# One core, two transformer blocks: convolution-branch gates ahead of the latents' up products

## The chip, the cores and the metric

The kernel runs on one core of one Trainium2 chip. Its time is the device time of one execution in microseconds (us). The engines are TensorE (PE; PEld is its weight load), VectorE (DVE), ScalarE (ACT), GpSimd (POOL) and SyncE (SP, which only issues DMAs here).

## What is computed

512 tokens of width 1024 go through two layers of a first block and then two layers of a second. The change is in the first block only:

```
def _layer(x, mem, positions, w_in, ...):
    proj = x @ w_in
    (aq, ak, av, ag, bcq, bckv, bkr, bg, cq, ck, cv, cg, mq, mg) = jnp.split(proj, _split_points(), axis=-1)
    ya = _banded_chunk_attention(aq, ak, av, A_PREV_CHUNKS, rel_bias=rel_bias)
    yb = _mla(bcq, bckv, bkr, positions, mla_q_norm, w_uq, mla_kv_norm, w_ukv)
    yc = _banded_chunk_attention(rope(cq), rope(ck), cv, SWA_PREV_CHUNKS, sinks=swa_sinks)
    ym = _memory_attention(mq, mem, w_mem_kv)
    gated = jnp.concatenate([ya * silu(ag), yb * silu(bg), yc * silu(cg), ym * silu(mg)], axis=-1)
    return _layer_norm(alpha * x + gated @ w_out, ln_gain, ln_bias)
```

`_mla` (branch B) normalises the latents `bcq` and `bckv`, multiplies them by `w_uq` and `w_ukv` (the up products), turns 32 of each query head's 96 rows by the rotary tables, and attends. Branch C is called the convolution branch in the change's title; its gate is `cg`, branch B's is `bg`.

## The kernel before

Everything is kept transposed (features on partitions, 512 tokens along the free axis). Each float32 product is three matmuls on a high and a low part (`r3`, line 554): a product of a 128x128 weight block with 512 tokens is one k part, 3 matmuls, and a projection tile of 128 features is 8 of them.

Weights come in chunks of two tiles. SP loads a chunk into one of two buffers `w_stage`, ACT rounds it into `w_hi` (line 1049, in halves), POOL makes `w_lo` (line 540, 8 pieces), and PE's `begin_chunk` waits for both. Chunks 10, 11 and 12 of a layer hold the up products' weights (`CHUNK_U`), the C gates (`CHUNK_CG`) and the B gates (`CHUNK_BG`).

Attention of a layer is a pipeline of 32 pairs of heads by query tile: steps 0 to 7 belong to branch A, 8 to 15 to M (memory), 16 to 23 to C, 24 to 31 to B, and two more steps drain it. In step t PE issues the scores of pair t (line 602), for every fourth step the spread of the head sums (line 640), the value products of pair t-2 (line 616), the transposes of pair t-1 (line 626), and then the step's share of other work. DVE takes the masked maximum of pair t (lines 1548, 1556 or 1553) and then copies the transposes of pair t-1 out of PSUM (line 1531); ACT takes the exponentials (line 1096). Scores of pair t need the PSUM bank that the copy of pair t-2 frees.

The other work is cut by hand into units: three in each of steps 0 to 3, two in each later step, so that step t above 3 has units 12 + 2(t - 4) and the one after. `b1_units` lists them; PE's, ACT's and DVE's `later_projections` are generators written to match. A number n in ACT's or DVE's `until(n)` means that what follows runs at unit n, behind that engine's attention work of the unit's step and ahead of that of the next step. All units' results go to two PSUM banks in turn, and PE's `acquire` waits until ACT (`evac`, line 1116) or DVE has taken what was there before.

Before the change the units are: cv up to 29; `uk` (keys of B) at 30 and 31, with the transposes of cv at 32; `uv` (values) 33 and 34; `uq` (queries) 35 and 36, one empty; `cg0`, `cg1` at 38 to 45 in quarters; `bg0`, `bg1` at 46 to 61 in eighths. The four rotations of the query heads (`rope`, lines 1505, 1507 and 1510, three DVE instructions for each head) run at units 41 and 42. Seven parts of the gated output are rounded and split (`split_out` on ACT, `out_lo` on DVE, lines 1112 and 1579) at units 62 to 65.

Of the kernel before, what the change touches and what calls it, by code (L numbers as in the profile page):

```python
# [20 lines left out]
P = 128  # L21
# [4 lines left out]
TT = TOK // P  # L26
# [36 lines left out]
def segments():  # L63
# [5 lines left out]
    for l in range(DEPTH):  # L69
# [7 lines left out]
        for n, (f0, nf) in enumerate(HALVES):  # L77
            early = 2 if n == 0 else 0
            if early:
# [9 lines left out]
              "bkv", "bq0", "bq1", "ck", "cq0", "cq1", "cv", None, None, None, "cg0", "cg1", "bg0", "bg1"]  # L89
AHEAD = 12  # L90
CHUNK_CQ, CHUNK_CV, CHUNK_U, CHUNK_CG, CHUNK_BG = 8, 9, 10, 11, 12
# [15 lines left out]
def b1_units(l):  # L107
# [139 lines left out]
def build(nc, dram, out):  # L247
# [3 lines left out]
    with ctx:  # L251
# [294 lines left out]
        def _(pe):  # L546
# [146 lines left out]
            def later_projections(l, c0):  # L693
# [36 lines left out]
                c = c0 + CHUNK_U  # L730
                begin_chunk(c)
                pe.wait_ge(S("lat_split"), 3 * l + 3)
                for h in range(4):
                    o = acquire(("uk", l, h))
                    w = slice(768 + h * 64, 768 + h * 64 + 64)
                    r3(o[0:64, :], w_hi[:, c % 2, w], w_lo[:, c % 2, w], lat_h[:, 2, :], lat_l[:, 2, :], True, True, True)
                    if h % 2 == 1:
                        yield
                transpose_all(("tv", l, "cv"), ("w", l, "cv"), qb[:, 2, :])
                yield  # L740
                for t in range(TT):
                    o = acquire(("uv", l, t))
                    w = slice(768 + 256, 768 + 512)
                    r3(o[:, 0:256], lat_h[:, 2, t * P:t * P + P], lat_l[:, 2, t * P:t * P + P], w_hi[:, c % 2, w], w_lo[:, c % 2, w],
                       True, True, True)
                    if t % 2 == 1:
                        yield
                for h in range(4):
                    o = acquire(("uq", l, h))
                    w = slice(h * 96, h * 96 + 96)  # L750
                    w1 = slice(384 + h * 96, 384 + h * 96 + 96)
                    r3(o[0:96, :], w_hi[:, c % 2, w], w_lo[:, c % 2, w], lat_h[:, 0, :], lat_l[:, 0, :], True, False)
                    r3(o[0:96, :], w_hi[0:64, c % 2, w1], w_lo[0:64, c % 2, w1], lat_h[0:64, 1, :], lat_l[0:64, 1, :], False, True, True)
                    if h % 2 == 1:
                        yield
                yield
                yield from pair_of_tiles(CHUNK_CG)
                yield from pair_of_tiles(CHUNK_BG, 8)
# [265 lines left out]
        def _(act):  # L1024
# [93 lines left out]
            for l in range(DEPTH):  # L1118
# [40 lines left out]
                def later_projections():  # L1159
# [45 lines left out]
                    for n in range(2):  # L1205
                        yield from until(30 + n)
                        round_chunk(b1_chunk(l, 11), half=n)
                        for h in (2 * n, 2 * n + 1):
                            evac(("uk", l, h), kb[0:64, h, :], rows=slice(0, 64))
                    yield from until(32)  # L1210
                    token_major(("tv", l, "cv"), vc[:, :, :])
                    for n in range(2):
                        yield from until(33 + n)
                        for t in (2 * n, 2 * n + 1):
                            evac(("uv", l, t), vb[:, t, :], cols=slice(0, 256))
                    for n in range(2):
                        yield from until(35 + n)
                        for h in (2 * n, 2 * n + 1):
                            evac(("uq", l, h), qb[0:96, h, :], rows=slice(0, 96), scale=SCALE_B)
# [878 lines left out]
```

## Time and profile before

| | us |
|---|---|
| three runs | 1737.13, 1739.89, 1739.97 (median 1739.89) |
| the profiled execution | 1740.3 |
| its span, first to last instruction | 1738.5 |
| attention of layer 0, first C scores to the output product | 190.55 to 263.83 |
| attention of layer 1, first C scores to the output product | 491.27 to 567.04 |
| PE busy share of the span | 96% |
| mean granted TensorE clock | 0.978 |

A timeline row gives start, duration, engine, line, operation, result and operands, the number of instructions that are merged in the row, and in brackets how long the engine had been idle and what released it. A matmul's own duration overlaps with the next one, so that work on PE is measured from start to start. A granted clock of 1.00 is TensorE's 2.4 GHz, 0.50 is 1.2 GHz.

### The profile page before, as it was taken

The numbers are of one execution on the slowest core, as the hardware profiler recorded it, in microseconds if no ns is written. First come the engines' busy times: TensorE is split into PE (matmuls) and PEld (weight loads), VectorE is DVE, ScalarE is ACT, GpSimd is POOL, SyncE is SP. The second block draws the span as 40 slices with busy tenths as digits, with TensorE's granted clock in tenths as the row PEclk, the third lists the DMA queues.
The fourth block names the chain that finished last, engine by engine and source line by source line (L and its number), as shares of the span: only waits on it lengthen the run. The fifth ranks groups of instructions, "written<-read, shape, count | busy, mean of one in ns | idle before, by whom it ended". The sixth has DMA issues, their size and how long they took to land.

```text
span 1738.5 us, 23836 instructions
## 1 busy us (share of the span) xinstructions
PE 1668.4 (96%) x8754; PEld 1320.4 (76%) x8754; DVE 786.5 (45%) x1498; ACT 695.0 (40%) x1146; POOL 683.6 (39%) x523
## 2 busy tenths in 40 slices
PE   6999899999999979989999999999998999999999
PEld 5777668787666857868888888888876888888887
DVE  7216664402666265673544115523665355404440
ACT  4344462633445153553433224333454344313431
POOL 3432315343231544425444444344352544344433
PEclk9999999999998979989999999999999999999999
DMA  6321203222120213112222232224221322232222
GB/s 248 107 80 49 80 25 122 96 100 74 50 75 26 85 49 103 51 50 97 97 97 78 91 108 88 91 79 138 86 74 41 105 77 94 90 103 97 97 81 88
DMA packets 26879, 150.68 MB, mean 87 GB/s; under 512 B 3888, under 2 KB 4144, under 8 KB 12912
## 3 DMA queue, kind: packets, MB, share of 16 engines
q1 hardware_dynamic: 23968, 142.78, 24.3%
q10 hardware_dynamic: 2832, 6.84, 1.1%
q8 instruction: 50, 0.82, 0.2%
q14 instruction: 29, 0.24, 0.0%
HBM read 142.66 MB, written 2.10 MB: 83 GB/s over the span
## 4 chain that ended last, share of the span: by engine, by line
PE 85%; DVE 6%; ACT 3%; issue 3%; POOL 2%; DMA 1%; ACTq 0%; DVEq 0%; POOLq 0%
PE ring L554 72%; PE outs L616 3%; PE scores L602 2%; PE ring L602 1%; POOL w_lo L540 1%; PE scores L626 1%; PE ring L640 1%; PE ring L626 1%; PE ring L670 1%; DMA xt<-in_x 1%; DVE tmp L1505 1%; POOL w_fold L532 1%; ACT xt L1267 1%; ACT w_hi L1049 1%; DVE probs_t L1531 0%
## 5 line engine op out<-in xcount | busy, mean ns | idle before, releaser
L540 POOL TENSOR_TENSOR w_lo<-w_stage,w_hi 128x258 fp32r<-128x258 f32 (+5 forms) x471 | 650.0, 1410 | 1010.8 <-ACT w_hi L1049 610.5
L554 PE MATMUL ring<-xh,w_lo 128*128 128x512 f32 x1296 | 519.6, 401 | 19.2 <-DVE w_lo L1463 10.7
L554 PE MATMUL ring<-xh,w_hi 128*128 128x512 f32 x1296 | 514.1, 397 | 0.0
L554 PE MATMUL ring<-xl,w_hi 128*128 128x512 f32 x1296 | 513.8, 396 | 0.0
L554 PEld LDWEIGHTS ring<-xh,w_lo 128*128 128x128 f32 x1296 | 245.5, 189 | 80.7 <-DVE w_lo L1463 10.7
L554 PEld LDWEIGHTS ring<-xh,w_hi 128*128 128x128 f32 x1296 | 246.1, 190 | 55.7
L554 PEld LDWEIGHTS ring<-xl,w_hi 128*128 128x128 f32 x1296 | 246.0, 190 | 53.3
L1394 ACT ACTIVATE w_hi<-w_stage 128x2048 fp32r<-128x2048 f32 (+2 forms) x70 | 116.6, 1666 | 158.2 <-PE ring L554 158.2
L1404 ACT ACTIVATE g<-ring,convw 128x512 f32<-128x512 f32 x88 | 68.1, 778 | 245.4 <-DVE ring L1903 245.4
L1049 ACT ACTIVATE w_hi<-w_stage 128x2064 fp32r<-128x2064 f32 (+2 forms) x81 | 123.4, 1536 | 64.9 <-PE ring L554 64.4
L1885 DVE TENSOR_TENSOR xt<-xt,ring 128x512 f32<-128x512 f32 x48 | 33.0, 688 | 247.3 <-PE ring L554 247.3
L554 PE MATMUL ring<-act_h,w_lo 128*128 128x512 f32 x352 | 139.2, 395 | 0.0
L1903 DVE TENSOR_TENSOR ring<-ring,tmp 128x512 f32<-128x512 f32 x88 | 61.2, 699 | 172.1 <-PE ring L554 161.9
L554 PE MATMUL ring<-act_h,w_hi 128*128 128x512 f32 x352 | 139.0, 395 | 0.0
L554 PE MATMUL ring<-act_l,w_hi 128*128 128x512 f32 x352 | 138.9, 395 | 0.0
L554 PEld LDWEIGHTS ring<-act_h,w_lo 128*128 128x128 f32 x352 | 66.3, 188 | 16.2 <-DVE act_l L1916 0.7
L1096 ACT ACTIVATE probs<-scores,neg_max 128x256 f32<-128x256 f32 (+2 forms) x96 | 50.2, 526 | 71.0 <-DVE neg_max L1550 14.3
L554 PEld LDWEIGHTS ring<-act_h,w_hi 128*128 128x128 f32 x352 | 66.2, 188 | 15.7
L554 PEld LDWEIGHTS ring<-act_l,w_hi 128*128 128x128 f32 x352 | 66.2, 188 | 15.7
L1096 ACT ACTIVATE probs<-ring,neg_max 128x256 f32<-128x256 f32 (+2 forms) x96 | 45.9, 481 | 72.4 <-DVE neg_max L1548 19.6
L1910 DVE SCALAR_TENSOR_TENSOR g<-ring,convw,g 128x511 f32<-128x511 f32 x88 | 66.0, 750 | 12.1 <-DVE g L1908 4.6
L1908 DVE SCALAR_TENSOR_TENSOR g<-ring,convw,g 128x511 f32<-128x511 f32 x88 | 65.2, 741 | 1.0 <-ACT g L1404 1.0
(281 smaller groups left out, 2213.4 us busy)
## 6 DMA issues: line engine op xcount, KB each, us to landing
w_stage<-in_mixed SPq DMA_DIRECT2D x62, 1032.0 KB, 4.8
w_stage<-in_up SPq DMA_DIRECT2D x44, 1024.0 KB, 4.8
w_stage<-in_down SPq DMA_DIRECT2D x16, 768.0 KB, 4.3
w_stage<-in_down SPq DMA_DIRECT2D x16, 640.0 KB, 3.9
xt<-in_x ACTq DMA_DIRECT2D x4, 512.0 KB, 11.4
g<-q SPq DMA_DIRECT2D x16, 128.0 KB, 2.3
out_t<-xt ACTq DMA_DIRECT2D x8, 256.0 KB, 2.0
mem_f<-in_mem SPq DMA_DIRECT2D x1, 1024.0 KB, 9.6
```

The source lines that it names most:

```text
L540: ins = nc.gpsimd.tensor_tensor(w_lo[:, slot, cols], source[:, cols], w_hi[:, slot, cols].bitcast(F32), ALU.subtract)
L554: ins = nc.tensor.matmul(o, lhs, rhs, start=start, stop=stop, skip_group_check=True)
L602: nc.tensor.matmul(acquire(("S", it["n"]))[:, 0:it["nb"] * P], q_of(it), k_of(it, l), start=True, stop=True, skip_group_check=True).then_i ...
L616: ins = nc.tensor.matmul(o_bank[it["o"] % 2][lo:lo + 64, it["qt"] * P:it["qt"] * P + P], v_of(it, l, j), probs_t[:, it["par"], j * P:j * P ...
L626: ins = nc.tensor.transpose(o[:, j * P:j * P + P], probs[:, it["n"] % 3, j * P:j * P + P], ident[:, :])
L1049: ins = A(w_hi[:, c % 2, first:last], source[:, first:last], ACT.Copy)
L1096: A(probs[:, n % 3, 0:w], bank(("S", n))[:, 0:w], ACT.Exp, bias=per_row(neg_max, it), scale=1.0 if it["branch"] == "M" else -1.0, accum_ou ...
L1394: A(w_hi[:, c % 2, 0:width], w_stage[:, c % 2, 0:width], ACT.Copy).then_inc(S("w_hi_done"), 1)
L1404: A(g[:, 4 * s + 2 + v, :], bank((kind, l, f0 + first + s))[:, :], ACT.Identity, bias=convw[:, l, taps, 4 * v + 3:4 * v + 4], scale=convw[ ...
L1903: v.tensor_tensor(bank(name)[:, :], bank(name)[:, :], tmp[:, 0, :], ALU.mult).then_inc(S("normed"), 1)
L1908: step(v.scalar_tensor_tensor(out=cc[:, 1:TOK], in0=hh[:, 0:TOK - 1], scalar=convw[:, l, i * 2 + (f0 + first + s), 4 * c:4 * c + 1], in1=c ...
L1910: v.scalar_tensor_tensor(out=cc[:, 0:TOK - 1], in0=hh[:, 1:TOK], scalar=convw[:, l, i * 2 + (f0 + first + s), 4 * c + 2:4 * c + 3], in1=cc ...
```

## The change

The C gates come ahead of the up products, and the chunks swap places in the weight stream. The units of the up products come in the order uq, uk, uv, one in every second unit with an empty one in front. The first B gate keeps its eighths, the second comes in quarters. There are 64 units where there were 62.

```
@@ the units
-              "bkv", "bq0", "bq1", "ck", "cq0", "cq1", "cv", None, None, None, "cg0", "cg1", "bg0", "bg1"]
+              "bkv", "bq0", "bq1", "ck", "cq0", "cq1", "cv", None, "cg0", "cg1", None, None, "bg0", "bg1"]
-CHUNK_CQ, CHUNK_CV, CHUNK_U, CHUNK_CG, CHUNK_BG = 8, 9, 10, 11, 12
+CHUNK_CQ, CHUNK_CV, CHUNK_CG, CHUNK_U, CHUNK_BG = 8, 9, 10, 11, 12
-    units += [[("uk", l, 0), ("uk", l, 1)], [("uk", l, 2), ("uk", l, 3)], [("tv", l, "cv")]]
-    for name in ("uv", "uq"):
-        units += [[(name, l, 0), (name, l, 1)], [(name, l, 2), (name, l, 3)]]
-    units += [[]]
+    units += [[("tv", l, "cv")], []]
     for t in ("cg0", "cg1"):
         units += [[], [], [], [("w", l, t)]]
-    for t in ("bg0", "bg1"):
-        units += [[]] * 7 + [[("w", l, t)]]
+    for name in ("uq", "uk", "uv"):
+        units += [[], [(name, l, 0), (name, l, 1)], [], [(name, l, 2), (name, l, 3)]]
+    units += [[]] * 7 + [[("w", l, "bg0")]] + [[]] * 3 + [[("w", l, "bg1")]]
@@ ACT
+                    yield from until(30)
                     token_major(("tv", l, "cv"), vc[:, :, :])
+                    yield from round_halves(32, b1_chunk(l, 11))
+                    yield from until(35)
                     evac(w("cg0"), g[:, 4, :])
-                    yield from until(45)
+                    yield from until(39)
                     evac(w("cg1"), g[:, 5, :], ACT.Silu)
+                    for n in range(2):
+                        yield from until(41 + 2 * n)
+                        for h in (2 * n, 2 * n + 1):
+                            evac(("uq", l, h), qb[0:96, h, :], rows=slice(0, 96), scale=SCALE_B)
+                        round_chunk(b1_chunk(l, 12), half=n)
+                    for n in range(2):
+                        yield from until(45 + 2 * n)
+                        for h in (2 * n, 2 * n + 1):
+                            evac(("uk", l, h), kb[0:64, h, :], rows=slice(0, 64))
+                    for n in range(2):
+                        yield from until(49 + 2 * n)
+                        for t in (2 * n, 2 * n + 1):
+                            evac(("uv", l, t), vb[:, t, :], cols=slice(0, 256))
+                    yield from round_halves(52, b1_chunk(l, 13))
                     for t in range(2):
-                        yield from until(53 + 8 * t)
+                        yield from until(59 + 4 * t)
                         evac(w(f"bg{t}"), g[:, 2 + t, :], ACT.Silu)
                     for n in range(7):
-                        yield from until(62 + n // 2)
+                        yield from until(64 + n // 2)
                         split_out(l, n)
@@ DVE
                     for h in range(4):
-                        yield from until(41 + h // 2)
+                        yield from until(46 + h // 2)
                         if h == 0:
                             dve.wait_ge(S("uq_swapped"), 32 * (l + 1))
                         rope(tmp[rr, h, :], qb[rr, h, :], rr, cos32, sin32, [qb[rr, h, :]], "rope_done")
                     for n in range(7):
-                        yield from until(62 + n // 2)
+                        yield from until(64 + n // 2)
                         out_lo(l, n)
```

PE's generator follows the same list; its arithmetic is the same, in another order. Lines of the changed kernel are up to 5 higher on DVE and ACT and 2 lower on PE.

On DVE, before, from the copy of pair 17 to the mask of pair 20 (steps 18 to 20 of layer 0):

```order
L1531 COPY probs_t<-scores 128x256 x2
L1679 TENSOR_TENSOR g<-outs,g 128x512
L1505 TENSOR_TENSOR tmp<-tmp,sin_67 32x512
L1507 TENSOR_TENSOR qb<-qb,cos_66 32x512
L1510 TENSOR_TENSOR qb<-qb,tmp 32x512
L1505 TENSOR_TENSOR tmp<-tmp,sin_67 32x512
L1507 TENSOR_TENSOR qb<-qb,cos_66 32x512
L1510 TENSOR_TENSOR qb<-qb,tmp 32x512
L1556 ISA scores,neg_max<-scores,masks,neg_sink 128x256
```

The same engine in the changed kernel, from the gate of branch C (`scale_gate`, now L1677) on, in step 21:

```order
L1677 TENSOR_TENSOR g<-ring,g 128x512
L1510 TENSOR_TENSOR tmp<-tmp,sin_67 32x512
L1512 TENSOR_TENSOR qb<-qb,cos_66 32x512
L1515 TENSOR_TENSOR qb<-qb,tmp 32x512
L1510 TENSOR_TENSOR tmp<-tmp,sin_67 32x512
L1512 TENSOR_TENSOR qb<-qb,cos_66 32x512
L1515 TENSOR_TENSOR qb<-qb,tmp 32x512
L1510 TENSOR_TENSOR tmp<-tmp,sin_67 32x512
L1512 TENSOR_TENSOR qb<-qb,cos_66 32x512
L1515 TENSOR_TENSOR qb<-qb,tmp 32x512
L1510 TENSOR_TENSOR tmp<-tmp,sin_67 32x512
L1512 TENSOR_TENSOR qb<-qb,cos_66 32x512
```

Units 46 and 47 are both in step 21, so that the rotations, which stood two and two around the mask of pair 19, now stand all four in a row, ahead of the mask of pair 22.

On PE, before, the end of step 15 of layer 0: the values and, right behind, the first query head, with the semaphores that each waits for (`ring_freed0` and `ring_freed1` are the two banks of the units):

```order
L554 MATMUL ring<-w_hi,lat_l 128x256 [waits ring_freed0]
L554 MATMUL ring<-w_lo,lat_h 128x256
L554 MATMUL ring<-w_hi,lat_h 128x256
L554 MATMUL ring<-w_hi,lat_l 128x256 [waits ring_freed1]
L554 MATMUL ring<-w_lo,lat_h 128x256
L554 MATMUL ring<-w_hi,lat_h 128x256
L554 MATMUL ring<-lat_h,w_lo 96x512 [waits ring_freed0]
```

The same engine in the changed kernel, the units of step 22 and the scores behind them:

```order
L552 MATMUL ring<-w_hi,lat_l 128x256 [waits ring_freed0]
L552 MATMUL ring<-w_lo,lat_h 128x256
L552 MATMUL ring<-w_hi,lat_h 128x256
L552 MATMUL ring<-w_hi,lat_l 128x256 [waits ring_freed1]
L552 MATMUL ring<-w_lo,lat_h 128x256
L552 MATMUL ring<-w_hi,lat_h 128x256
L600 MATMUL scores<-kc,qc 128x256 [waits ring_freed4]
```

The query heads no longer follow the values; what follows is the scores of pair 23, which wait for DVE's copy of pair 21 (`ring_freed4`).

On ACT, before, the end of the attention (from the exponential of pair 28 on):

```order
L1096 ACTIVATE probs,row_sum<-ring,neg_max 128x128 x2
L1116 ACT_TABLE_LOAD
L1116 ACTIVATE g<-ring 128x512
L1096 ACT_TABLE_LOAD
L1096 ACTIVATE probs,row_sum<-scores,neg_max 128x256 x2
L1112 ACTIVATE xh<-g 128x512 x4
L1096 ACTIVATE probs,row_sum<-ring,neg_max 128x384 x2
L1112 ACTIVATE xh<-g 128x512 x3
L1096 ACTIVATE probs,row_sum<-scores,neg_max 128x512 x2
```

The same engine in the changed kernel, from the exponential of pair 28 on:

```order
L1101 ACTIVATE probs,row_sum<-ring,neg_max 128x128 x2
L1101 ACTIVATE probs,row_sum<-scores,neg_max 128x256 x2
L1121 ACT_TABLE_LOAD
L1121 ACTIVATE g<-ring 128x512
L1101 ACT_TABLE_LOAD
L1101 ACTIVATE probs,row_sum<-ring,neg_max 128x384 x2
L1117 ACTIVATE xh<-g 128x512 x4
L1101 ACTIVATE probs,row_sum<-scores,neg_max 128x512 x2
```

The last gate with its two table loads and the four splits have moved behind one more exponential, a step later.

## Rows read from the trace of the kernel before

**Rows 1.** The page, part 1: busy time of each engine

```profile
PE 1668.4 (96%) x8754; PEld 1320.4 (76%) x8754; DVE 786.5 (45%) x1498; ACT 695.0 (40%) x1146; POOL 683.6 (39%) x523
```

**Rows 2.** Waits of PE, 430 to 610: total, times, longest

```profile
PE ring L554 <- ACT vc L1154: 0.3, 1, 0.3
```

**Rows 3.** Timeline of PE, layer 1: waits in steps 13 to 21

```profile
477.71 0.44 PE L554 MATMUL ring<-lat_h,w_lo 128*64 128x512 f32 x1 [0.54 <-DVE g L1672]
488.35 0.48 PE L554 MATMUL ring<-lat_h,w_lo 128*96 128x512 f32 x1 [2.08 <-ACT vb L1116]
511.64 0.82 PE L602 MATMUL ring<-kc,qc 64*128 64x128 f32 x4 [1.04 <-DVE probs_t L1531]
517.31 1.03 PE L602 MATMUL scores<-kc,qc 64*128 64x256 f32 x4 [0.89 <-DVE probs_t L1531]
```

**Rows 4.** Timeline of PE, layer 1: steps 13 to 23

```profile
480.14 0.70 PE L602 MATMUL ring<-km,qm 64*128 64x256 f32 x4
...
485.32 0.36 PE L554 MATMUL ring<-w_hi,lat_l 128*128 128x256 f32 x1
...
519.92 0.48 PE L554 MATMUL ring<-xh,w_lo 128*128 128x512 f32 x1
...
521.49 0.70 PE L602 MATMUL ring<-kc,qc 64*128 64x256 f32 x4
...
522.90 0.48 PE L554 MATMUL ring<-xh,w_lo 128*128 128x512 f32 x1
...
524.47 0.70 PE L602 MATMUL scores<-kc,qc 64*128 64x256 f32 x4
```

**Rows 5.** Timeline of DVE, layer 1: the four rotations and the gate

```profile
504.49 0.95 DVE L1505 TENSOR_TENSOR tmp<-tmp,sin 32x512 f32<-32x512 f32 x1
...
510.25 0.49 DVE L1556 CUSTOM_DVE_ANT_0 scores<-scores,masks,neg_sink 128x256 f32<-128x256 f32 x1
...
511.17 0.75 DVE L1531 COPY probs_t<-ring 128x256 f32<-128x256 f32 x2
511.95 0.68 DVE L1505 TENSOR_TENSOR tmp<-tmp,sin 32x512 f32<-32x512 f32 x1
...
515.90 0.36 DVE L1556 CUSTOM_DVE_ANT_0 ring<-ring,masks,neg_sink 128x128 f32<-128x128 f32 x1
...
520.50 0.68 DVE L1672 TENSOR_TENSOR g<-ring,g 128x512 f32<-128x512 f32 x1
```

**Rows 6.** Timeline of POOL, layer 1: the weight split beside those rotations

```profile
501.37 6.97 POOL L540 TENSOR_TENSOR w_lo<-w_stage,w_hi 128x258 fp32r<-128x258 f32 x8 [14.16 <-ACT w_hi L1049]
```

**Rows 7.** Timeline of PE, layer 1: from step 30 to the output product

```profile
550.05 1.56 PE L602 MATMUL ring<-kb,qb 96*128 96x384 f32 x4 [0.28 <-DVE probs_t L1531]
...
554.76 3.06 PE L602 MATMUL scores<-kb,qb 96*128 96x512 f32 x4 [2.19 <-DVE probs_t L1531]
...
561.08 1.55 PE L616 MATMUL outs<-probs_t,vb 128*64 128x128 f32 x12 [0.74 <-DVE probs_t L1531]
...
567.04 0.50 PE L554 MATMUL ring<-xh,w_lo 128*128 128x512 f32 x1
```

**Rows 8.** Timeline of DVE, layer 1: four splits of the output

```profile
550.88 2.50 DVE L1579 TENSOR_TENSOR xl<-g,xh 128x512 fp32r<-128x512 f32 x4
```

**Rows 9.** Timeline of PE, layer 0: the same end of the attention

```profile
249.34 1.56 PE L602 MATMUL ring<-kb,qb 96*128 96x384 f32 x4 [0.28 <-DVE probs_t L1531]
...
254.05 2.73 PE L602 MATMUL scores<-kb,qb 96*128 96x512 f32 x4 [2.19 <-DVE probs_t L1531]
...
263.83 0.50 PE L554 MATMUL ring<-xh,w_lo 128*128 128x512 f32 x1
```

**Rows 10.** Stretches: busy time of each engine, then the granted clock

```profile
255.00:260.00 5.00, 4.14 (x20) 2.09 (x19) 4.35 (x10) 2.58 (x6) 0.00 (x0) 0.66 0.00 0
483.00:488.00 5.00, 3.13 (x25) 2.29 (x25) 4.92 (x8) 1.75 (x8) 4.22 (x5) 1.00 0.02 3
553.00:558.00 5.00, 3.24 (x6) 1.08 (x8) 4.91 (x12) 2.79 (x7) 0.00 (x0) 0.75 0.00 0
558.00:563.00 5.00, 4.26 (x28) 3.23 (x27) 2.16 (x7) 1.56 (x4) 0.00 (x0) 0.50 0.02 3
563.00:568.00 5.00, 5.00 (x44) 4.31 (x43) 2.77 (x4) 0.08 (x1) 0.00 (x0) 0.72 0.00 0
```

More of the change, by code:

```diff
@@ L728, in later_projections @@
                 yield from tile("cv", 4, c, lambda k: slice(k * P, k * P + P))
[L730 to L738, printed above, removed]
@@ L739, in later_projections @@
                 transpose_all(("tv", l, "cv"), ("w", l, "cv"), qb[:, 2, :])
                 yield
[L741 to L755, printed above, removed]
@@ L756, in later_projections @@
                 yield
                 yield from pair_of_tiles(CHUNK_CG)
-                yield from pair_of_tiles(CHUNK_BG, 8)
+                c = c0 + CHUNK_U
+                for n in range(2):
+                    yield
+                    if n == 0:
+                        begin_chunk(c)
+                        pe.wait_ge(S("lat_split"), 3 * l + 3)
+                    for h in (2 * n, 2 * n + 1):
+                        o = acquire(("uq", l, h))
+                        w = slice(h * 96, h * 96 + 96)
+                        w1 = slice(384 + h * 96, 384 + h * 96 + 96)
+                        r3(o[0:96, :], w_hi[:, c % 2, w], w_lo[:, c % 2, w], lat_h[:, 0, :], lat_l[:, 0, :], True, False)
+                        r3(o[0:96, :], w_hi[0:64, c % 2, w1], w_lo[0:64, c % 2, w1], lat_h[0:64, 1, :], lat_l[0:64, 1, :], False, True, True)
+                    yield
@@ L760, in u_tile @@
+                c = c0 + CHUNK_BG
+                begin_chunk(c)
+                for t, parts in ((0, 8), (1, 4)):
+                    yield from tile(f"bg{t}", parts, c, lambda k: slice(k * 256 + t * P, k * 256 + t * P + P))
             def u_tile(l, c, t, ch, halves=False):
@@ L1204, in later_projections @@
                     evac(w("cv"), qb[:, 2, :])
[L1205 to L1210, printed above, removed]
-                    token_major(("tv", l, "cv"), vc[:, :, :])
[L1212 to L1219, printed above, removed]
-                    yield from round_halves(38, b1_chunk(l, 12))
-                    yield from until(41)
+                    yield from until(30)
+                    token_major(("tv", l, "cv"), vc[:, :, :])
+                    yield from round_halves(32, b1_chunk(l, 11))
+                    yield from until(35)
                     evac(w("cg0"), g[:, 4, :])
-                    yield from until(45)
+                    yield from until(39)
                     evac(w("cg1"), g[:, 5, :], ACT.Silu)
@@ L1226, in later_projections @@
                     A(g[:, 4, :], g[:, 4, :], ACT.Silu).then_inc(S("gates_ready"), 1)
-                    yield from round_halves(46, b1_chunk(l, 13))
+                    for n in range(2):
+                        yield from until(41 + 2 * n)
+                        for h in (2 * n, 2 * n + 1):
+                            evac(("uq", l, h), qb[0:96, h, :], rows=slice(0, 96), scale=SCALE_B)
+                        round_chunk(b1_chunk(l, 12), half=n)
+                    for n in range(2):
+                        yield from until(45 + 2 * n)
+                        for h in (2 * n, 2 * n + 1):
+                            evac(("uk", l, h), kb[0:64, h, :], rows=slice(0, 64))
+                    for n in range(2):
+                        yield from until(49 + 2 * n)
+                        for t in (2 * n, 2 * n + 1):
+                            evac(("uv", l, t), vb[:, t, :], cols=slice(0, 256))
+                    yield from round_halves(52, b1_chunk(l, 13))
                     for t in range(2):
-                        yield from until(53 + 8 * t)
+                        yield from until(59 + 4 * t)
                         evac(w(f"bg{t}"), g[:, 2 + t, :], ACT.Silu)
                     for n in range(7):
-                        yield from until(62 + n // 2)
+                        yield from until(64 + n // 2)
                         split_out(l, n)
```

11 lines of the change are left out of this document (added).

## The prediction, made before the changed kernel had run

> **What bounds the kernel now.** I read the page first. PE is busy for 96% of the span and no other engine for half of it [rows 1]: the kernel ends when PE has done its work, and a change that leaves PE's work as it is can only move PE's waits and its clock. So I looked at PE's waits inside the attention stage, where the change lies, and then at the timeline of PE, DVE and POOL around each, to see what comes before and behind it. The two layers run this stage alike; I work with layer 1 and count it twice.
>
> Five waits lie where units move [rows 2, 3]. The second key head waits 0.54 us for a bank that DVE's gate multiplication still holds; the second value tile 0.3 for the copy of cv; the first query head 2.08, because it follows the values at once and ACT, in its order, takes them only behind the exponential of pair 15. The scores of pairs 20 and 21 wait 1.04 and 0.89 for the copies of pairs 18 and 19, which DVE does only behind two rotations each. The reader is to see in the DVE rows that two rotations run from 504.49 to the mask at 510.25 and two from 511.95 to the mask at 515.90 [rows 5]: 5.76 us while POOL splits weights (501.37 to 508.34 [rows 6]), 3.95 without it.
>
> **What goes.** No unit of the up products follows another at once any more: the query heads stand at units 41 and 43, so that ACT has a step's time to take each pair, and no rotation is left at units 41 and 42. All five waits go: 0.3 + 0.54 + 2.08 + 1.04 + 0.89 = 4.85 us a layer. The number of matmuls, exponentials, table loads, roundings and DMAs stays; PE's work costs nothing more and nothing less. SP: the chunk behind `CHUNK_U` and the swap of query halves still leave behind the last query head. That head is taken at about unit 43, in step 19, and the rotations come at the end of step 21. Two steps lie between, so the swap is hidden.
>
> **What comes: four rotations in a row.** Units 46 and 47 are both in step 21, so DVE does four rotations between the gate of C and the mask of pair 22. What is queued behind them is that mask, then the copy of pair 21, and the scores of pair 23 on PE wait for this copy. I count from the first unit of step 21 on PE (519.92 before [rows 4]).
> - DVE: the gate is done at 520.50 + 0.68, so 1.26 after it. Four rotations are twice 3.95 = 7.9. The two masks take 511.17 - 510.25 = 0.92 [rows 5], the first copy half of 0.75. The bank is free at 1.26 + 7.9 + 0.92 + 0.38 = 10.46.
> - PE: in that step it now has two key heads instead of a part of bg0. Three heads took 480.14 - 477.71 = 2.43 [rows 3, 4], so 0.81 each; the second waits for the gate's bank until 1.3 and ends at 2.1. Step 22 up to its unit is 522.90 - 521.49 = 1.41 [rows 4]. Two value tiles follow: they start at 485.32 and the query head behind them is late by 2.08 at 488.35 [rows 3, 4], so 0.95. PE is ready for pair 23 at 2.1 + 1.41 + 0.95 = 4.5.
>
> The new wait is 10.46 - 4.5 = 5.9 us. Step 22 cannot cover it, since its other unit is empty: that is the price of small units between large ones. POOL's split of the chunk behind ends about when the rotations start (its second half is rounded behind the last query head, two steps before; the split is 7 us [rows 6]); so I take the rate without it, and the other rate, 5.76 for two, as the upper bound.
>
> Smaller new waits, which no row shows as such. The scores of pair 14 follow after only the transposes of cv, and the copies of pair 12 are not done: 0.35, between nothing and 0.75 (one double copy [rows 5]). The fourth key head waits for the gate: 0.5, by the same wait of 0.54 before [rows 3]. Pair 24, the first of B, stands right behind the last values, which ACT takes behind two exponentials: 0.5, between nothing and the 2.08 that this pattern cost before. Together 5.9 + 0.35 + 0.5 + 0.5 = 7.25. Against 4.85 that is +2.4 a layer up to B.
>
> **The end of the attention.** Six k parts of bg0, which lay in steps 21 to 23, now lie behind the start of B, and steps 28 and 29 get the fuller units. Two such parts, six matmuls, take 524.47 - 522.90 = 1.57 [rows 4]. This is work moved, and its sum is the same: B starts earlier by what left. In step 29 it covers the 0.28 before pair 30 and the short gap ahead of it: -0.5. The wait of 2.19 at pair 31 [rows 7, 9] is there because DVE does four splits (2.50 [rows 8]) ahead of the mask of pair 30. These now stand one step later, ahead of the mask of pair 31. So the 2.19 nearly goes, but the copy of pair 30 is late instead: the value product that waited 0.74 waits about 2 us more, and the last gate's table loads and the rest of the splits sit on ACT and DVE behind it. I take -0.5 for this exchange, between -2 and +1. Sum a layer: +2.4 - 0.5 - 0.5 = +1.4, for two +2.8.
>
> **The clock.** Behind the 2.19 of each layer's end the granted clock fell to 1.2 GHz: 0.66 over 255 to 260, and 0.75, 0.50, 0.72 over 553 to 568. Over 483 to 488, with 3.13 us of work in 5, it stayed at 2.4 GHz [rows 10]. At half speed 5 x 0.34 = 1.7 us of clock were lost in layer 0, and 5 x (0.25 + 0.50 + 0.28) = 5.1 in layer 1. Not all of it shows: from pair 30 to the output product layer 1 takes 567.04 - 550.05 = 16.99, layer 0 14.49 [rows 7, 9], so 2.5 of the difference of 3.4 do. With about 0.5 in layer 0, where DVE sets the pace, the low clock costs some 0.5 + 3.0 = 3.5 now. A wait of 5.9 is more than twice what brought the clock down. I put it at 2.0 a layer, near the 1.7 of the shorter case, with 0 and 5.1 as bounds; and for the end of the attention, where the wait is as long as before, 1.5 a layer instead of 3.5 for both. That is 4.0 + 3.0 - 3.5 = +3.5.
>
> The Trainium skill, "TensorE: Matmul & The Clock Gate", section "Why this matters for your kernels", advises against idle gaps of TensorE between bursts of matmuls, since the clock goes back to half behind one. By that the new wait costs the clock in both layers; by the row of 483 to 488 alone it would cost nothing, and the sum would be 4.0 lower. The trace agrees with the page at both ends of the attention.
>
> **Sum.** 2.8 + 3.5 = +6.3 on the profiled execution's 1740.3, so 1746.6. The median of the runs is 0.4 below that execution: 1746.2, rounded to 1746.
>
> **Rivals.**
> - *The same wait, but the clock stays up or is soon back.* For: DVE or ACT pace the steps behind it, so a slow PE is partly hidden, as in layer 0's end. Against: 5.9 us is long. Time: 1739.9 + 2.8 - 0.5 = 1742, down to 1739.5 if the low clock of the ends goes too.
> - *The rotations are contended.* If POOL's split of the next chunk runs beside them, four take 2 x 5.76 = 11.5 instead of 7.9: +3.6 a layer, 1753. For: the one pair of rotations that had POOL beside it was that slow [rows 5, 6]. Against: by my walk POOL ends about where they start; a start of POOL 3 us later decides it.
> - *The wait is covered, and the kernel is faster.* If PE comes to the scores of pair 23 no earlier than DVE has copied pair 21, the 5.9 goes with its 2.0 of clock: 1746.2 - 2 x 7.9 = 1730. It decides where the new wait is under about 2 us: 5.9 - 2.0 would have to be hidden. For: the order puts a step of PE's work between gate and scores. Against: this step holds 3.2 us of work and the rotations 7.9 by the rows; PE has nothing else to do before pair 23.
>
> **How the numbers follow.** A measurement of this kernel tells about 0.2% (3.5 us) from no change. The forecast (slower, 1743.5 to 1750) gets 0.58, the clock rival 0.20, the contended one 0.12, the covered one 0.10. The range of 1739.5 to 1753 takes in the first two and half of the third; with the bounds of the clock (0 and 5.1 a layer) it would be wider on top, and those ends are unlikely. Slower: the forecast and the contended case, less the forecast's low edge, 0.68. Within 0.2%: 0.20. Faster: the covered case, and the clock rival with both ends at full clock, 0.12.
>
> **What would show it.** In the changed profile the waits of rows 2 and 3 are gone; the scores of pair 23 wait some 6 us for DVE's copy in each layer, with twelve rotation instructions in a row on DVE and a granted clock of 0.50 behind; pair 31 waits under 1 us and the value product of pair 30 some 2 to 3. I am wrong if the rotations take less than 7 us or far more, if PE's wait there is under 4 us, if the clock stays at 1.00 behind it, or if the clock's low stretches elsewhere (the layer norms) change by as much as this sum.

## The result: 0.4% slower

| | us |
|---|---|
| before | 1740.93 median (1737.13 to 1746.45, 11 runs) |
| after | 1749.72 median (1744.16 to 1752.10, 11 runs) |
| ratio | 1.0040, 95% interval 1.0026 to 1.0055 |
| profiled executions | 1740.3 and 1746.1, spans 1738.5 and 1744.2 |

The page of the changed kernel (part 1, answers to [rows 1]) shows the same work: PE is as busy and has as many instructions.

```profile
PE 1666.6 (96%) x8754; PEld 1321.2 (76%) x8754; DVE 782.3 (45%) x1498; ACT 695.9 (40%) x1146; POOL 680.9 (39%) x523
```

Waits of PE, layer 1, 420 to 620 (total, times, longest). None of the five of [rows 2, 3] is left; one of 6.6 has come:

```profile
PE scores L600 <- DVE probs_t L1536: 7.7, 3, 6.6
PE outs L614 <- DVE probs_t L1536: 2.6, 1, 2.6
...
PE ring L600 <- ACT vb L1121: 1.2, 1, 1.2
PE ring L552 <- DVE g L1677: 0.4, 1, 0.4
```

Timeline of PE, layer 0: the fourth key head, the last value tile, pair 23, pair 24, and at the end pair 31, the value product of pair 30 (answers to [rows 4, 9]):

```profile
210.06 0.44 PE L552 MATMUL ring<-lat_h,w_lo 128*64 128x512 f32 x1 [0.38 <-DVE g L1677]
...
212.99 0.28 PE L552 MATMUL ring<-w_hi,lat_h 128*128 128x256 f32 x1
219.90 1.55 PE L600 MATMUL scores<-kc,qc 64*128 64x256 f32 x4 [6.64 <-DVE probs_t L1536]
...
226.03 1.20 PE L600 MATMUL ring<-kb,qb 96*128 96x128 f32 x4 [1.21 <-ACT vb L1121]
...
256.88 1.98 PE L600 MATMUL scores<-kb,qb 96*128 96x512 f32 x4 [0.30 <-DVE probs_t L1536]
...
262.89 0.88 PE L614 MATMUL outs<-probs_t,vb 128*64 128x128 f32 x12 [2.64 <-DVE probs_t L1536]
```

Between 213.2 and 219.9 PE has nothing; layer 1 has the same 6.64. DVE in layer 1, from the gate to the mask of pair 22 (answers to [rows 5]), with POOL's split:

```profile
515.88 0.68 DVE L1677 TENSOR_TENSOR g<-ring,g 128x512 f32<-128x512 f32 x1
516.60 0.82 DVE L1510 TENSOR_TENSOR tmp<-tmp,sin 32x512 f32<-32x512 f32 x1
517.35 1.22 DVE L1512 TENSOR_TENSOR qb<-qb,cos 32x512 f32<-32x512 f32 x1
518.60 0.68 DVE L1515 TENSOR_TENSOR qb<-qb,tmp 32x512 f32<-32x512 f32 x1
...
525.08 0.49 DVE L1561 CUSTOM_DVE_ANT_0 ring<-ring,masks,neg_sink 128x256 f32<-128x256 f32 x1
```

```profile
511.96 6.05 POOL L538 TENSOR_TENSOR w_lo<-w_stage,w_hi 128x258 fp32r<-128x258 f32 x8 [19.75 <-ACT w_hi L1054]
```

The twelve instructions take 525.08 - 516.60 = 8.48 us. The first two are slower (0.82 and 1.22), while POOL still splits (to 518.01); the other ten take 0.68. The Trainium skill, "SBUF — State Buffer", section "Who interferes with whom", says that a VectorE instruction with both inputs in SBUF contends with a GpSimd instruction that reads SBUF. The trace agrees: 0.82 and 1.22 beside POOL, 0.68 without it.

Stretches of the changed kernel (busy time of PE, PEld, DVE, ACT, POOL, then the granted clock; answers to [rows 10]):

```profile
210.00:215.00 5.00, 3.21 (x21) 1.99 (x21) 4.90 (x8) 0.90 (x2) 1.45 (x2) 1.00 0.47 165
215.00:220.00 5.00, 0.10 (x1) 0.10 (x1) 4.88 (x12) 0.86 (x4) 0.00 (x0) 0.64 0.11 46
220.00:225.00 5.00, 4.83 (x22) 3.55 (x22) 2.58 (x8) 2.74 (x12) 0.00 (x0) 0.50 0.00 0
225.00:230.00 5.00, 3.97 (x19) 3.25 (x20) 1.79 (x8) 1.31 (x6) 0.00 (x0) 0.50 0.00 0
...
525.00:530.00 5.00, 3.53 (x17) 2.55 (x18) 3.52 (x13) 2.36 (x9) 0.00 (x0) 0.50 0.00 0
530.00:535.00 5.00, 3.79 (x28) 3.15 (x28) 2.16 (x10) 2.94 (x11) 0.00 (x0) 0.96 0.00 2
```

The granted clock falls during the wait (0.64 in the stretch that ends with it). Behind the wait PE works at 1.2 GHz, in layer 0 for all of 220 to 230, in layer 1 for little more than 525 to 530.

To place the time in every kernel that follows I read three starts on PE's timeline in each layer: the first scores of M (step 8), the first of B (step 24) and the output product. "M to B" and "B to output" are their differences, layer 0 / layer 1, from the profiled execution of each kernel. The medians come from several rounds, in which the kernel before had 1739.6 to 1741.9; each ratio further down compares within its round.

| kernel | median of runs | M to B | B to output |
|---|---|---|---|
| before | 1740.9 | 80.02 / 80.03 | 36.96 / 39.47 |
| after | 1749.7 | 80.48 / 80.02 | 42.27 / 40.34 |
| e1_one_a_step | 1745.8 | 79.71 / 79.66 | 40.39 / 40.32 |
| e2_filled_wait | 1741.9 | 78.66 / 78.63 | 40.52 / 39.67 |
| e3_before_batched | 1757.6 | 91.81 / 89.04 | 37.69 / 37.75 |
| e4_no_rotation | 1726.8 | 71.71 / 71.74 | 39.72 / 39.67 |
| e5_before_no_rotation | 1740.2 | 77.20 / 81.86 | 37.03 / 39.53 |
| e6_before_one_a_step | 1738.6 | 77.68 / 77.79 | 39.40 / 39.41 |
| e7_before_gap_moved | 1735.7 | 77.53 / 77.61 | 39.49 / 39.39 |
| e8_splits_early | 1750.4 | 79.96 / 80.39 | 41.40 / 45.53 |
| e9_packed_rotation | 1741.8 | 77.16 / 76.63 | 42.06 / 40.33 |
| e10_two_and_two | 1748.1 | 78.73 / 78.66 | 42.12 / 44.35 |
| e11_packed_early | 1730.1 | 72.77 / 72.64 | 43.26 / 39.68 |

Six bg0 parts of a layer moved from the first stretch to the second, so only the sum of the two compares kernels of the two orders. After less before it is +5.77 and +0.86. That is 6.6; the start of layer 0's attention, 1.3 us earlier in this execution (99.43 against 100.73), takes some back, and the spans differ by 5.7. The medians differ by 8.8: the profiled execution of the changed kernel is the second shortest of its eleven runs, with a mean granted clock of 0.977 where six of the others had 0.971 to 0.973. The 3 us between are in executions of which there is no trace.

### The profile page after: what moved, and what is told of

The parts are those of the page before. It is cut to its first block, busy times and chain, and to the rows that moved or that the text cites. A ratio compares the mean times of both kernels' runs of the same rounds, so it can differ in the third digit from the quotient of the medians.

```text
span 1744.2 us, 23836 instructions
## 1 busy us (share of the span) xinstructions
PE 1666.6 (96%) x8754; PEld 1321.2 (76%) x8754; DVE 782.3 (45%) x1498; ACT 695.9 (40%) x1146; POOL 680.9 (39%) x523
## 4 chain that ended last, share of the span: by engine, by line
PE 88%; DVE 5%; ACT 3%; issue 2%; POOL 1%; DMA 1%; ACTq 0%; DVEq 0%; POOLq 0%
PE ring L552 74%; PE outs L614 3%; PE scores L600 2%; PE ring L600 2%; PE scores L624 2%; PE ring L638 2%; PE ring L624 1%; PE ring L668 1%; POOL w_lo L538 1%; DMA xt<-in_x 1%; ACT xt L1272 1%; DVE tmp L1510 0%; DVE g L1758 0%; PE ring L677 0%; DVE xt L1715 0%
## 5 line engine op out<-in xcount | busy, mean ns | idle before, releaser
L1101 ACT ACTIVATE probs<-ring,neg_max 128x256 f32<-128x256 f32 (+2 forms) x96 | 45.9, 481 | 72.2 <-DVE neg_max L1553 20.3
```

The lines of the kernel that those rows point to most:

```text
L1101: A(probs[:, n % 3, 0:w], bank(("S", n))[:, 0:w], ACT.Exp, bias=per_row(neg_max, it), scale=1.0 if it["branch"] == "M" else -1.0, accum_ou ...
```

## Experiments

The theory: the four rotations in one batch are the loss, by the wait that they make and the low clock behind it, and the moved units by themselves are a gain. The rivals are that the moved gates, the small new waits and the end of the attention are the loss, or that the clock costs nothing, since DVE sets the pace there.

**Without the rotations, in both kernels**

```
-                        rope(tmp[rr, h, :], qb[rr, h, :], rr, cos32, sin32, [qb[rr, h, :]], "rope_done")
+                        dve.sem_inc(S("rope_done"), 1)
```

> The changed kernel without the rotary turn of B's four query heads (left out in both layers; the swap of halves is still made). It measures all that the rotations cost where they stand. The batch theory expects 2 x 6.64 of wait and the clock gone, and the small waits left: 14 to 19 us below the changed kernel, 1730 to 1735. The rival that the moved gates and the small new waits are the price expects it no lower than the kernel before less what its own rotations cost there (2 x 1.93): 1737 or above.

> The kernel before without the rotary turn of B's four query heads (left out in both layers; the swap of halves is still made). Beside the changed kernel without it (1726.8 us, so 23 below the changed kernel) it tells what the moved units alone are worth. The theory that the rotations' place is all of the loss expects the kernel before to lose less by it, its two waits of 1.04 and 0.89 a layer: 1740.3 - 3.9 - 0 to 2 of later steps = 1734 to 1737, and so above 1726.8: the moved units alone are then a gain of 7 to 10 us. The rival that the moved gates are a price expects it below 1726.8.

Measured: the changed kernel 1726.8 (ratio to before 0.9916, 0.9896 to 0.9935), 22.9 below the changed kernel by the medians, 21.6 by the ratios, and so more than the 14 to 19 that I expected; the kernel before 1740.2 (0.9992, 0.9972 to 1.0011), no different from itself. In the changed kernel M to B is 8.77 and 8.28 shorter, so the batch is worth more than its wait of 6.64. In the kernel before it is 2.82 shorter in layer 0, but 1.83 longer in layer 1. There the old wait at the first query head stands as it did, and this time the clock fell behind it (two stretches of e5_before_no_rotation first, then the same of the kernel before):

```profile
485.00:490.00 5.00, 2.91 (x10) 1.60 (x9) 2.17 (x5) 1.57 (x6) 1.43 (x2) 0.75 0.48 163
490.00:495.00 5.00, 5.00 (x20) 2.86 (x18) 0.75 (x5) 1.54 (x4) 0.00 (x0) 0.50 0.11 48
```

```profile
485.00:490.00 5.00, 2.92 (x16) 1.86 (x16) 2.92 (x6) 1.57 (x6) 2.22 (x2) 1.00 0.33 92
490.00:495.00 5.00, 5.00 (x30) 3.11 (x30) 1.50 (x7) 2.21 (x7) 0.00 (x0) 1.00 0.28 119
```

Behind the wait of 2.09 layer 1 of e5 loses 81.86 - 77.20 = 4.7 us against its own layer 0; behind the same wait of 2.08 the kernel before loses nothing (80.03 and 80.02). So 1740.2 is above what I expected, and the 13.4 between the two kernels without rotations holds clock as well as layout. In layer 0, where neither has that low clock, both stretches together are 114.23 and 111.43, so the kernel with the moved units is 2.8 shorter. Part of this is clock too, at the end of the attention: e5 has low clock there, e4 has none.

```profile
250.00:255.00 5.00, 3.62 (x8) 1.37 (x10) 4.90 (x13) 2.85 (x8) 0.00 (x0) 0.70 0.00 0
255.00:260.00 5.00, 4.12 (x49) 3.25 (x46) 2.92 (x7) 1.50 (x4) 0.00 (x0) 0.96 0.00 0
```

Counted as in the prediction, 5 x (0.30 + 0.04) = 1.7 us at most are lost there. The moved units alone are then a gain of 1.1 to 2.8 in this layer; e4's waits there are 1.0 shorter in sum. The first rival falls: without the rotations the moved units cost nothing. What the batch costs is split into wait and clock below.

**The batch alone, in the kernel before**

```
-                        yield from until(41 + h // 2)
+                        yield from until(46 + h // 2)
```

> The kernel before with its four rotations in one step (21) instead of two each in steps 18 and 19; units and gates stay where they are. It is the batch alone. The batch theory expects the waits of 1.04 and 0.89 at pairs 20 and 21 gone and a wait of 5 to 7 us at pair 23 in each layer, less what step 21's and 22's parts of bg0 cover beyond the changed kernel's units, and a low clock behind: +3 to +5 a layer of wait and 1 to 2 of clock, 1749 to 1755. The rival that the moved units are the price expects it near the kernel before, within 3 us of 1741.

Measured: 1757.6, ratio 1.0105 (1.0078 to 1.0131): 17 us, more than I gave either theory. Timeline of its PE, then of its DVE and POOL, layer 0:

```profile
232.33 1.55 PE L602 MATMUL scores<-kc,qc 64*128 64x256 f32 x4 [9.80 <-DVE probs_t L1531]
```

```profile
219.20 0.68 DVE L1505 TENSOR_TENSOR tmp<-tmp,sin 32x512 f32<-32x512 f32 x1
...
224.02 1.21 DVE L1505 TENSOR_TENSOR tmp<-tmp,sin 32x512 f32<-32x512 f32 x1
225.16 1.21 DVE L1507 TENSOR_TENSOR qb<-qb,cos 32x512 f32<-32x512 f32 x1
226.41 1.10 DVE L1510 TENSOR_TENSOR qb<-qb,tmp 32x512 f32<-32x512 f32 x1
...
230.94 0.49 DVE L1556 CUSTOM_DVE_ANT_0 ring<-ring,masks,neg_sink 128x256 f32<-128x256 f32 x1
```

```profile
221.16 9.21 POOL L540 TENSOR_TENSOR w_lo<-w_stage,w_hi 128x258 fp32r<-128x258 f32 x8 [13.38 <-ACT w_hi L1049]
```

Here POOL splits a chunk beside the batch, which takes 230.94 - 219.20 = 11.74 and not 8.5. It is the contended rival of the prediction, with its 11.5, in the other kernel. Not all of the 17 us is the batch: in layer 0 the granted clock also fell behind the old wait of 2.07 at the first query head (0.81 and 0.51 over 185 to 195), and "M to B" is 2.8 longer there than in layer 1, where it did not.

**The clock without the wait**

```
+                        for _ in range(16 if t == 1 else 0):
+                            r3(o[:, 0:256], lat_h[:, 2, t * P:t * P + P], lat_l[:, 2, t * P:t * P + P],
+                               w_hi[:, c % 2, w], w_lo[:, c % 2, w], True, True)
```

> The changed kernel with the second value tile's three matmuls issued 16 times more in step 22 of each layer, the same product again, so that PE works where it waited for DVE's copy of pair 21; nothing else is changed. It separates the clock from the wait. The clock theory expects the scores of pair 23 at the same time as before (DVE sets it), a clock of 1.00 behind, and so a gain over the changed kernel of what the low stretch costs: some 1 to 2 us in layer 1 (6.8 us of low clock) and 2 to 4 in layer 0 (13.7 us), 3 to 6 in all, so 1743 to 1746. The rival that the low clock is hidden by DVE and ACT expects no difference (within 1 us). If the filling is longer than the wait, the row shows PE busy until the scores and the excess is to be taken off.

Measured: 1741.9, ratio 1.0006 (0.9992 to 1.0020) where the changed kernel has 1.0040. Pair 23 in layer 0, and stretches of e2_filled_wait:

```profile
219.97 1.03 PE L600 MATMUL scores<-kc,qc 64*128 64x256 f32 x4 [0.92 <-DVE probs_t L1539]
```

```profile
215.00:220.00 5.00, 4.08 (x36) 3.87 (x34) 4.88 (x12) 0.79 (x3) 0.00 (x0) 1.00 0.13 54
220.00:225.00 5.00, 3.56 (x28) 2.73 (x30) 2.66 (x9) 2.84 (x12) 0.00 (x0) 1.00 0.00 0
```

Pair 23 still starts when DVE lets it, 74.32 us behind the first scores of M and 74.35 in the changed kernel, so the filling changed the clock and not the time at which PE goes on. The clock stays at 1.00 there, and the two stretches of a layer together are 3.57 and 2.06 shorter: 5.6 us (5.2 in the spans, 5.9 by the ratios, 7.8 by the medians). Of this 0.7 is the end of layer 1's attention, where e2 has 1.00 and the changed kernel 0.80 and 0.86, so the low clock behind the two waits costs 5.0. The rival that DVE hides it falls. Repeated matmuls in the wait made the changed kernel faster.

With e4 this splits the batch's cost. In layer 1, e2 has a granted clock of 1.00 from M to the output product and so has e4, and e2 takes 118.30 where e4 takes 111.41: 6.9 us a layer are delay alone, 13.8 for both. The low clock behind the waits is 5.0, that at the ends of the attention 1.5. Together this is the 20.3 by which the changed kernel's two layers are longer than e4's.

**The same rotations, spread**

```
e1:   until((44, 46, 48, 50)[h])       changed kernel, steps 20 to 23
e10:  until(46 + 2 * (h // 2))         changed kernel, two in step 21, two in step 22
e6:   until(41 + 2 * h)                kernel before, steps 18 to 21
```

> The changed kernel with its four rotations of a layer one in each of steps 20 to 23 (units 44, 46, 48, 50) instead of all in step 21. The batch theory (the 6.64 us wait at the scores of pair 23 and the low clock behind it are the price of the change) expects no wait over 2 us there, a granted clock of 1.00 behind it, and 1.3 + 6.64 x 2 less small new waits of some 1 to 2 us a step: 8 to 14 us below the changed kernel, so 1736 to 1742, at or below the kernel before. The rival that the moved gates and the end of the attention are the price expects the large wait gone too, but the time within 3 us of the changed kernel's 1749. The rival that rotations always cost PE their time, wherever they stand, expects two or more waits of 2 to 3 us a layer in place of the one.

> The changed kernel with two of its four rotations in step 21 and two in step 22 (units 46 and 48). The theory that DVE is what steps 21 to 23 wait for, whichever way its 8.5 us are cut, expects a wait of about 2.6 at pair 23 (6.64 less two rotations of 2.05) and one of 2 to 4 at pair 24, their sum near the 6.64 + 1.21 of the changed kernel, and from the first scores of M to pair 24 again about 79 to 80 us; what it can give is some of the clock: 1742 to 1748. The rival that only the size of the single wait counts expects pair 24 2 us or more earlier, and 1738 or less.

> The kernel before with its four rotations one in each of steps 18 to 21 (units 41, 43, 45, 47) instead of two in each of steps 18 and 19. If what counts is how much of DVE's time stands between two copies that PE waits for, the waits of 1.04 and 0.89 at pairs 20 and 21 shrink to under 0.3 each and nothing new over 1 us comes, as steps 18 to 21 hold full tiles: 2 to 4 us below the kernel before, 1736 to 1738. The rival that any rotation in a step costs PE about 1 us expects 1740 with four waits a layer. In the changed kernel one a step gave waits of 4.12 (fourth key head, for the gate behind a rotation) and 2.81 (pair 24, for the last rotation); here pair 24 is two steps further off and no unit takes the gate's bank, so neither should come.

Measured: e1 1745.8 (1.0027, 1.0014 to 1.0040), e10 1748.1 (1.0033, 1.0013 to 1.0053), e6 1738.6 (0.9983, 0.9968 to 0.9997). e1 missed what I expected (1736 to 1742); e10 and e6 came out less than 1 us above theirs (1742 to 1748, 1736 to 1738). PE of e1, and its first rotation on DVE, layer 0:

```profile
215.18 0.69 PE L552 MATMUL ring<-lat_h,w_lo 128*64 128x512 f32 x1 [4.12 <-DVE g L1677]
...
226.63 0.68 PE L600 MATMUL ring<-kb,qb 96*128 96x128 f32 x4 [2.81 <-DVE qb L1515]
```

```profile
209.86 0.95 DVE L1510 TENSOR_TENSOR tmp<-tmp,sin 32x512 f32<-32x512 f32 x1 [2.79 <-DMA tmp<-qb]
```

and e10's:

```profile
217.65 1.55 PE L600 MATMUL scores<-kc,qc 64*128 64x256 f32 x4 [2.79 <-DVE probs_t L1536]
225.87 1.20 PE L600 MATMUL ring<-kb,qb 96*128 96x128 f32 x4 [3.30 <-ACT vb L1121]
```

4.12 + 2.81 = 6.9 and 2.79 + 3.30 = 6.1, beside 6.64 + 1.21 = 7.9 in the changed kernel. The 4.12 of e1 is not the rotation's time alone: DVE stood 2.79 us for the DMA that swaps the query halves, which comes late for a rotation in step 20, and that rotation then ran beside POOL (3.26 us to the next mask). So e1 doesn't tell what four single rotations cost; e10 has no such DMA wait, and with it 8.5 us in two parts lose nearly what they lose in one: pair 24 comes 1.4 to 1.8 us sooner, under the 2 of the rival. In steps 21 to 23, with half their units empty, PE has too little work to cover them. In the full steps of e6 there is no wait at pairs 20 and 21, nor another over 0.3 in its place: M to B is 2.3 shorter in both layers. The gain comes out smaller in the total, as the end of the attention in layer 0 has more low clock (39.40 against 36.96).

**The gap moved, and the splits moved back**

```
e7 = e6 and:  uk uk tv uv uv uq uq []   ->   uk uk tv uv uv [] uq uq
e8:           until(64 + n // 2)        ->   until(62 + n // 2)       on ACT and DVE, changed kernel
```

> The kernel before with one rotation a step, as in the run beside it, and with its one empty unit moved from behind the query heads to between the values and the query heads (they stand at units 36 and 37 instead of 35 and 36); everything else stays. The wait of 2.08 a layer at the first query head, which follows the values at once, should go or fall under 0.5; up to 0.5 a layer may come at pair 17, as a step gets two query units less or more. Expected: 2 to 4 us below the run beside it, 1733 to 1735. The rival that ACT is simply late in these steps expects the wait of about 2 to show at the second query unit or at the first part of cg0 instead, and no gain.

> The changed kernel with the splits of the outputs (ACT's high parts and DVE's low parts) from unit 62 on, as in the kernel before, instead of 64. It tests the exchange at the end of the attention alone. If it is an exchange, the wait of 0.30 at pair 31 grows to about 2.2 and the 2.64 of pair 30's value product falls to about 0.8, and the time stays within 2 us of the changed kernel in each direction; the low clock at the end can change by up to 5 us in one layer either way. The rival that the later splits are a cost expects 3 us or more below the changed kernel.

e7: 1735.7 (0.9960, 0.9946 to 0.9975), where I expected 1733 to 1735. The wait of 2.08 is gone, but pair 16 waits 1.49 instead (187.34, for a copy of DVE), and M to B gains only 0.15 a layer: a wait exchanged for one. That its median is 2.8 under e6's is in no stretch that I read: the profiled spans are 1735.4 for e7 and 1734.7 for e6. Its cause stays open.

e8: 1750.4 (1.0046, 1.0030 to 1.0063), no different from the changed kernel. Layer 0, pair 31 and the value product of pair 30:

```profile
258.54 3.17 PE L600 MATMUL scores<-kb,qb 96*128 96x512 f32 x4 [2.81 <-DVE probs_t L1536]
264.43 0.88 PE L614 MATMUL outs<-probs_t,vb 128*64 128x128 f32 x12 [0.88 <-DVE probs_t L1536]
```

3.7 in place of 0.30 + 2.64 = 2.9. The exchange at the end is one, and small. Layer 1 of this trace has "B to output" at 45.53 against 40.34, and the reason is clock: behind the same 6.64 at pair 23 it stayed low for longer, and it fell again at the end (0.64 and 0.68 over 565 to 575).

```profile
525.00:530.00 5.00, 3.67 (x18) 2.69 (x19) 3.55 (x12) 2.49 (x9) 0.00 (x0) 0.50 0.00 0
530.00:535.00 5.00, 3.79 (x20) 2.98 (x20) 1.38 (x8) 1.81 (x8) 0.00 (x0) 0.50 0.01 2
535.00:540.00 5.00, 5.00 (x22) 3.91 (x22) 1.64 (x5) 2.74 (x5) 1.63 (x3) 0.59 0.00 0
```

This execution took 1750.7, near both medians; the changed kernel's profiled one took 1746.1. What the trace of a kernel shows of the clock is one execution's.

**DVE's work in the batch cut to a quarter**

A rotation turns 32 partitions and takes as long as one over 128 would. The Trainium skill, "VectorE: DVE Perf Modes", section "Why `tensor_reduce` can't reduce along partition axis", says that each of the 128 partition lanes is a pipeline of its own and streams along the free dimension. By that, four heads' rows stacked in 128 partitions need three instructions instead of twelve.

```
@@ SP, behind the query heads (e9: all four taken first; e11: each head as soon as it is taken)
+  sp.dma_start(tmp[32 * h:32 * h + 32, 0, :], qb[64:96, h, :])
+  for a, b in ((0, 16), (16, 0)):
+      sp.dma_start(tmp[32 * h + a:32 * h + a + 16, 1, :], qb[64 + b:80 + b, h, :])
@@ DVE, unit 46
+  rope(tmp[:, 1, :], tmp[:, 0, :], full, cos32, sin32, [tmp[:, 2, :]], "rope_done")
@@ back, for each head (e9: ACT, unit 48; e11: SP)
+  dma_start(qb[64:96, h, :], tmp[32 * h:32 * h + 32, 2, :])
```

> The changed kernel with the four rotary turns of B's query heads done at once: their 32 rows each are brought by DMA into one tile of 128 partitions (heads one below the other, once as they are and once with the halves swapped), turned by three instructions over 128 partitions instead of twelve over 32, and brought back by four DMAs from ACT's queue; TensorE waits for these. If DVE's time in the batch is the whole price, as the run without rotations says (1726.8 us), this gives nearly all of it back: 3 x 0.68 = 2.0 us of DVE instead of 8.5, the wait at pair 23 gone or under 1 us, no low clock behind it, 1727 to 1732. The rival that the DMAs' way there and back is the next wait (the queries leave at unit 43 and are wanted at pair 24, about 14 us later by the trace of the changed kernel without rotations; each way is 2 to 4 us) expects a wait of 2 to 5 us a layer at pair 24 or at the mask of pair 22, and 1734 to 1745.

> The packed rotation once more, with its DMAs issued elsewhere. In the run before, SP issued its twelve only behind the last query head, 0.6 us each (204.32 to 211.79), so that DVE waited 3.37 us for the last, and the four back cost ACT 1.96 us ahead of the values' copies. Now each head's three leave as soon as that head is taken (six of them two steps earlier), and SP issues the four back itself. If the issues were what was left, DVE turns right behind the gate, the wait of 3.32 at pair 23 falls under 1 us and the low clock behind it goes: first scores of M to pair 24 in 72 to 74 us instead of 77.2, 1728 to 1733. The rival that the way back is too long expects a wait of 2 us or more at pair 24 for the four DMAs, and 1735 or more; the weight chunk behind them on SP leaves 3 to 5 us later, which should cost nothing, since it is wanted more than 20 us later.

e9: 1741.8 (1.0001, 0.9983 to 1.0019). Its DVE and its SP queue, layer 0:

```profile
209.12 0.68 DVE L1683 TENSOR_TENSOR g<-ring,g 128x512 f32<-128x512 f32 x1
213.17 0.69 DVE L1517 TENSOR_TENSOR tmp<-tmp,sin 128x512 f32<-128x512 f32 x1 [3.37 <-DMA tmp<-qb]
```

```profile
204.32 0.51 SPq L471 DMA_DIRECT2D tmp<-qb  x1
204.88 1.23 SPq L473 DMA_DIRECT2D tmp<-qb  x2
...
210.57 1.22 SPq L473 DMA_DIRECT2D tmp<-qb  x2
```

The instruction over 128 partitions takes 0.69 where one over 32 took 0.68, so the trace agrees with the Trainium skill. But SP issues its twelve DMAs one behind the other, 0.6 us each, and DVE waits for the last: the rival's case, at the mask of pair 22. PE still waits 3.32 at pair 23. With the issues earlier and off ACT:

e11: 1730.1 (0.9933, 0.9907 to 0.9958), 19.6 below the changed kernel and 0.7% below the kernel before. Its DVE, and its PE at pairs 23 and 24, layer 0:

```profile
211.52 0.93 DVE L1515 TENSOR_TENSOR tmp<-tmp,sin 128x512 f32<-128x512 f32 x1
...
215.52 1.03 PE L605 MATMUL scores<-kc,qc 64*128 64x256 f32 x4 [0.66 <-DVE probs_t L1541]
219.91 0.68 PE L605 MATMUL ring<-kb,qb 96*128 96x128 f32 x4 [1.48 <-ACT vb L1126]
```

DVE turns right behind the gate, the wait at pair 23 is 0.66, and M to B is within 1.1 of the kernel without rotations. In layer 0 the clock was still low for a part of the rest (0.68 over 220 to 225, 0.59 and 0.73 over 255 to 265), which is where its "B to output" of 43.26 comes from; layer 1 has 39.68, as without rotations.

## Why the prediction was right

**The time and the sign.** I said 1746; the profiled execution took 1746.1, and the medians lie 8.8 apart where I had 6.3. The forecast case came, with the mechanism that it gave, but the sum is partly luck. The waits of the attention grew by about 6.0 us for both layers (3.0 a layer, all waits of 0.25 us and more in the timelines together), where I had 2.8. The two layers grew by 6.6 in all, so that the clock's net share, by difference, is under 1 where I had 3.5. The two errors cancel. That the profiled execution fits to 0.1 is luck as well: it lies 3.6 below its median.

**What goes.** All five waits, as said.

**The wait at pair 23.** 5.9 predicted, 6.64 in both layers. The mechanism was right. Of the difference, 0.6 is the batch, 8.48 and not 7.9: POOL did not end "about when the rotations start" but 1.4 us later, and the first two instructions ran beside it. With POOL beside most of it, the price is e3's: 11.74 us.

**The small waits.** The fourth key head 0.36 to 0.38 (0.5 predicted), pair 24 1.21 (0.5), pair 14 none (0.35). Their sum is 1.6 where I had 1.35.

**The end of the attention.** Pair 31's wait went to 0.30, the value product's rose to 2.64, as the rows should show. I took -1.0 a layer for both terms; the waits there were 0.28 + 2.19 + 0.74 = 3.2 in layer 1 [rows 7] and are 2.9, so in waits it is -0.3. The clock there is the next point.

**The clock.** This was the term with the widest bounds, and it was mis-sized on both sides. Behind the new wait I took 4.0; the filled wait shows 5.0 in the traces (3.6 in layer 0, 1.4 in layer 1). For the ends of the attention I took 3.0 now and 3.5 before. In the changed kernel they cost 1.5 against e4, which has 1.00 there; and layer 1, which had lost more there than layer 0 [rows 10], lost little: 565 to 575 has 0.80 and 0.86 where 553 to 568 had 0.75, 0.50 and 0.72. If the net is under 1, the low clock cost the kernel before about 6, not 3.5; no run shows that kernel's ends at full clock, so this is by difference only. Why layer 1 lost so little now is shown by no run; the wait there is no shorter than before (2.64 and 2.19). Which of these waits is followed by low clock, and for how long, changes from one kernel to the next without anything near them having changed, as the old wait of 2.08 showed. Such a term has a size of some us that no walk through the trace gives.

**The rivals.** The covered wait (1730) did not come: step 21 and 22 hold what the rows said. The same wait without low clock (1742) is what e2 made, at 1741.9; that the numbers agree so closely is chance, since the waits in the rival's sum are 3 us too small. The contended batch (1753) came in e3, at 1757.6.

## What to carry to other kernels

Before moving small work of an engine into one place, sum what that engine must do between two results that the bounding engine waits for, and set it against the bounding engine's own work in the same steps: 8.5 us of DVE against half-empty steps of PE made waits of 6 to 8 us a layer, in one batch or in two. In the kernel before, steps full of PE's work covered one rotation each. In the changed kernel, the cure was to make the work smaller (stack partial-partition operands into all 128 partitions) and to start its DMAs as soon as each piece is ready. And a reordering whose total is a small loss may hold a gain and a larger loss: taking the suspected cost out in both orders shows both, if the clock's share is read from the stretches and taken off.

## What the runs showed of the hardware that I had not expected

- The low clock behind a wait costs a good part of the wait again: 5.0 us behind two waits of 6.64 (3.6 and 1.4), and filling the wait with repeated matmuls gave it back (e2). How long the clock stays low behind the same wait differs: 220 to 230 in one layer, little more than 525 to 530 in the other, and in e8's second layer nearly all of 525 to 540.
- A wait of 2.1 was followed by a granted clock of 1.00 in one execution (the kernel before) and of 0.75, 0.50, 0.73 in another (e5), at 4.7 us.
- DMA issues on one queue are serial at about 0.6 us each, whether the DMA carries 16 or 32 rows of 2 KB (twelve from 204.32 to 211.79 in e9); on ACT three of them took 1.89 us, which ACT's next instruction waited for.
- A VectorE instruction beside a split on POOL took 1.10 to 1.23 where it takes 0.68 alone, and POOL's split took 9.21 where another, without the rotations beside it, took 5.60 (e3).
